# Where four weight blocks and the activations lie in SBUF, modulo 512 bytes

## The chip, the cores and the metric

The kernel runs on one core of a Trainium2 chip. The metric is the device time of one execution in microseconds. The kernel before took 2354.36 us, the median of three runs (2339.87 to 2354.72 us).

## What is computed

Two layers of an encoder over 512 positions of width 1024, all in float32. Each layer adds four sub-layers to x, each between an RMS norm ahead and one behind:

```python
x = x + 0.5 * rms_norm(swiglu(rms_norm(x, g[FFN1_PRE]), ffn_w_in[l, 0], ffn_w_out[l, 0]), g[FFN1_POST])
...
y = concat(rms_norm(ya), rms_norm(yb), rms_norm(yc))   # neighbourhood attention, Hyena, dilated attention
x = x + rms_norm(y @ w_out[l], g[MIX_POST])
xa = memory_cross_attn(rms_norm(x, g[XA_PRE]), rms_norm(mem, g[XA_MEM]), xa_wq[l], xa_wkv[l], xa_wo[l])
x = x + rms_norm(xa, g[XA_POST])
x = x + 0.5 * rms_norm(swiglu(rms_norm(x, g[FFN2_PRE]), ffn_w_in[l, 1], ffn_w_out[l, 1]), g[FFN2_POST])
```

The SwiGLU layers have 2816 hidden units; their weights and those of the projections are most of the work and all of the traffic that matters.

## The kernel before, in words

**Products in two parts.** The large products are made with float32r operands, each number split into a high part and the rest: high by high, low by high and high by low are summed in PSUM. ScalarE writes the high part of a weight block (`high`, line 306), VectorE subtracts it for the low part (`low`, line 311).

**The ring.** Weights arrive by DMA as blocks of 128 partitions by 1024 columns in `raw0` and `raw1`. They are split into `wh0` to `wh3` and `wl0` to `wl3`, a ring of four blocks: unit `u` uses block `u % 4`. A layer has 116 units. TensorE's `unit_done` frees a block for ScalarE, `split_ready` hands it to TensorE.

**Which operand is which.** In the first products of a stage (lines 453 to 455, and `products`, lines 397, 399 and 401, as `unit` calls it) 128 columns of a block are the stationary operand and 256 columns of `uH` or `uL` move. In the group loop of the two SwiGLU layers' first product (lines 501 to 503, `factor_product`) the hidden units are made in groups of two by seven quarter products: the groups' sums of weights are split into blocks 0, 1, 2 (two products each) and 3 (one product) counted from the stage's base, which is block 0 of the ring in the first FFN of a layer and block 2 in the second. The moving operand is `uH`, `uL` or one of `T1` to `T4`. In the output products (`out_tile`, which calls `products` twice with 512 columns, done as two halves of 256) it is the other way round: 128 columns of `hs` or `uH` are stationary and the block moves. `memory_values` has `memH` and `memL` stationary and a block moving. Each matmul instruction loads its stationary operand anew.

**Other matmuls.** The remaining ones, transposes against `eye` and the attention and Hyena products, are plain float32. Line 617 is apart: `KEEP_BUSY` matmuls whose result nobody reads multiply 128 columns of a block by 512 columns of the same block.

**Where things lie.** Tensors are allocated in order of the code, from low addresses to high, each start rounded up to 32 bytes where it is not there already. `xs`, `raw`, `wh`, `wl`, `tmp` (12,288 bytes of a partition), `side` (4096), then small ones: `stat`, two `yb` of 2048, `rsm`, `ones` (512), `eye` (512), `epsc`, `pr`, `negmax`, `den` and `rden` (256 each), `gss` (192). Then `gain_rows` (8192), `uH`, `uL` and a region of 90,112 bytes that the stages share and lay out anew: `hs`, `T1H` to `T4L`, `memH` and the attention's tensors all start a multiple of 512 bytes from `uH`. `pr` holds 106 columns of parameters and `ALIGN` columns that nobody uses; `ALIGN` is 106 before, so `pr` has 848 bytes.

The engines are synchronised by semaphores written out by hand; the order of the instructions of each engine is fixed in the code, and the two group loops run as hardware loops.

Of the kernel before, what the change touches and what calls it, by code (L numbers as in the profile page):

```python
# [10 lines left out]
F32R = mybir.dt.float32r  # L11
AX = mybir.AxisListType

P = 128
LAYERS = 2
D = 1024
# [41 lines left out]
RING, RAWS = 4, 2  # L58
# [4 lines left out]
IT_A, IT_C, IT_X, ITEMS = 0, 24, 48, 64  # L63
# [6 lines left out]

G0, CW0, CB0, SK0, NPAR = 0, 80, 98, 104, 106

ALIGN = 106
PRE = (0, 2, 5, 8)
POST = (1, 4, 7, 9)
G_GROUP, G_MEM = 3, 6
# [4 lines left out]
def build(nc, x, mem, par, grow, w_first, w_second, w_proj, rpb, t5, fw1, fw23, fw4, fvec, decay,  # L81
          k_emb, k_fwd, k_inv, k_time, k_namask, k_hot, k_lnn, k_eye, out):
    with ExitStack() as ctx:
        def sb(name, shape, dt=F32):
            return ctx.enter_context(nc.sbuf_tensor(name, shape, dt))
# [6 lines left out]

        xs = sb("xs", [P, NT, D])
        raw = [sb(f"raw{i}", [P, D]) for i in range(RAWS)]
        wh = [sb(f"wh{i}", [P, D], F32R) for i in range(RING)]
        wl = [sb(f"wl{i}", [P, D], F32R) for i in range(RING)]
        work = sb("tmp", [P, 6 * T])
        tmp = [work[:, i * T:i * T + T] for i in range(6)]
        yg = work[:, 0:D]
# [7 lines left out]
        eye = sb("eye", [P, P])  # L107
        epsc = sb("epsc", [P, 2])
        pr = sb("pr", [P, NPAR + ALIGN])
        negmax = sb("negmax", [P, ITEMS])  # L110
        den = sb("den", [P, ITEMS])
        rden = sb("rden", [P, ITEMS])
        gss = sb("gss", [P, 3, GROUPS])
# [1927 lines left out]
```

## Time and profile before

| | |
|---|---|
| median of 3 runs | 2354.36 us |
| lowest, highest | 2339.87, 2354.72 us |
| the profiled execution | 2339.08 us |
| its span, first to last instruction | 2337.3 us |
| granted TensorE clock, mean | 0.999 |
| matmuls | 19,236 |
| DMA, mean rate | 101 GB/s |

The span and what lies around it differ by 1.8 us. All terms are worked out against this one execution. TensorE's matmul durations in the profile overlap, since matmuls are pipelined and their ends are modelled: a stretch's length over the number of matmuls that start in it is the pace, and the recorded duration is that pace and a constant.

### The profile page before, as it was taken

How to read it: one execution, taken by the hardware profiler on the slowest of the kernel's cores; microseconds unless marked ns; L12 is line 12 of the kernel's file. 1: busy time of each engine (PE TensorE's matmuls, PEld its weight loads, DVE VectorE, ACT ScalarE, POOL GpSimd, SP SyncE). 2: the span in 40 equal slices, each digit the busy share in tenths (PEclk: the TensorE clock that was granted, in tenths of full speed). 3: DMA queues.
4: the chain of work that ended last, by engine and by line, in shares of the span. 5: the costliest groups of instructions: out<-in, count | busy, mean ns of one | idle time of the engine just before them, and what ended most of it. 6: DMA issues, size and time to landing. Idle time of an engine off the chain costs nothing.

```text
span 2337.3 us, 46573 instructions
## 1 busy us (share of the span) xinstructions
PE 2311.4 (99%) x19236; PEld 2251.4 (96%) x19236; DVE 1559.7 (67%) x2175; ACT 1051.6 (45%) x1733; POOL 114.6 (5%) x185
## 2 busy tenths in 40 slices
PE   7999999999999999999999999999999999999998
PEld 7999999998999999999999999989989989999998
DVE  7999437535365499993499983565364554999833
ACT  5445335227453464452454442442384444544422
POOL 0000000610000000000000000016000000000000
PEclk9999999999999999999999999999999999999999
DMA  4333323340234133333233332234202431322332
GB/s 140 109 114 122 116 82 135 82 138 19 73 118 136 55 109 110 120 110 94 71 128 113 119 109 91 93 121 124 90 1 85 146 114 46 125 102 100 113 98 75
DMA packets 66258, 236.54 MB, mean 101 GB/s; under 512 B 8882, under 2 KB 10632, under 8 KB 65600
## 3 DMA queue, kind: packets, MB, share of 16 engines
q1 hardware_dynamic: 57600, 209.74, 26.8%
q0 software_dynamic: 8224, 24.12, 3.2%
q8 instruction: 110, 1.80, 0.3%
q10 hardware_dynamic: 288, 0.59, 0.1%
q14 instruction: 36, 0.29, 0.0%
HBM read 232.29 MB, written 2.12 MB: 100 GB/s over the span
## 4 chain that ended last, share of the span: by engine, by line
PE 96%; ACT 1%; DVE 1%; issue 1%; DMA 0%; DVEq 0%; SPq 0%; ACTq 0%
PE bank L397 14%; PE bank L399 14%; PE bank L401 14%; PE bank L501 11%; PE bank L502 11%; PE bank L503 11%; PE bank L654 3%; PE bank L453 3%; PE bank L455 2%; PE bank L454 2%; PE bank L629 2%; PE bank L725 1%; PE bank L438 1%; PE bank L584 1%; PE bank L607 1%
## 5 line engine op out<-in xcount | busy, mean ns | idle before, releaser
L311 DVE TENSOR_TENSOR wl<-raw,wh 128x1024 fp32r<-128x1024 f32 x232 | 287.7, 1240 | 379.2 <-ACT wh L306 378.7
L306 ACT ACTIVATE wh<-raw 128x1024 fp32r<-128x1024 f32 x232 | 245.2, 1057 | 545.8 <-PE bank L401 474.4
L397 PE MATMUL bank<-wh,hs 128*128 128x256 f32 x1408 | 279.1, 279 | 0.1
L399 PE MATMUL bank<-wl,hs 128*128 128x256 f32 x1408 | 278.4, 279 | 0.0
L401 PE MATMUL bank<-wh,hs 128*128 128x256 f32 x1408 | 278.0, 278 | 0.0
L501 PE MATMUL bank<-uH,wh 128*128 128x256 f32 x960 | 266.5, 278 | 0.0
L503 PE MATMUL bank<-uH,wl 128*128 128x256 f32 x960 | 266.3, 277 | 0.0
L502 PE MATMUL bank<-uL,wh 128*128 128x256 f32 x960 | 266.3, 277 | 0.0
L397 PEld LDWEIGHTS bank<-wh,hs 128*128 128x128 f32 x1408 | 214.2, 188 | 0.6 <-issue 0.6
L401 PEld LDWEIGHTS bank<-wh,hs 128*128 128x128 f32 x1408 | 214.3, 188 | 0.0
L399 PEld LDWEIGHTS bank<-wl,hs 128*128 128x128 f32 x1408 | 214.1, 188 | 0.0
L1361 DVE TENSOR_TENSOR wl<-S,wh 128x1024 fp32r<-128x1024 f32 x160 | 194.5, 1216 | 0.0
L501 PEld LDWEIGHTS bank<-uH,wh 128*128 128x128 f32 x960 | 181.2, 189 | 0.9 <-issue 0.9
L503 PEld LDWEIGHTS bank<-uH,wl 128*128 128x128 f32 x960 | 180.3, 188 | 0.0
L502 PEld LDWEIGHTS bank<-uL,wh 128*128 128x128 f32 x960 | 180.2, 188 | 0.0
L952 ACT ACTIVATE wh<-S 128x1024 fp32r<-128x1024 f32 x80 | 85.2, 1065 | 157.7 <-DVE S L1349 136.4
L397 PE MATMUL bank<-uH,wh 128*128 128x256 f32 x768 | 154.5, 283 | 0.0
L399 PE MATMUL bank<-uL,wh 128*128 128x256 f32 x768 | 152.2, 280 | 0.0
L401 PE MATMUL bank<-uH,wl 128*128 128x256 f32 x768 | 152.1, 280 | 0.0
L453 PE MATMUL bank<-uH,wh 128*128 128x256 f32 x512 | 145.6, 284 | 3.3 <-DVE uL L1276 3.3
L454 PE MATMUL bank<-uL,wh 128*128 128x256 f32 x512 | 143.3, 280 | 0.0
L455 PE MATMUL bank<-uH,wl 128*128 128x256 f32 x512 | 143.3, 280 | 0.0
(268 smaller groups left out, 6068.8 us busy)
## 6 DMA issues: line engine op xcount, KB each, us to landing
raw<-in_w_proj SPq DMA_DIRECT2D x128, 512.0 KB, 3.5
raw<-in_w_first SPq DMA_DIRECT2D x96, 512.0 KB, 3.7
raw<-in_w_second SPq DMA_DIRECT2D x88, 512.0 KB, 3.5
side<-in_w_first SPq DMA_DIRECT2D x40, 512.0 KB, 3.6
raw_value<-in_w_first SPq DMA_DIRECT2D x40, 512.0 KB, 4.3
gain_rows<-in_grow POOLq DMA_DIRECT2D x15, 512.0 KB, 4.8
strip<-bias_of_distance POOLq DMA_DIRECT2D x2, 2688.0 KB, 11.0
strip<-in_rpb POOLq DMA_DIRECT2D x96, 24.0 KB, 2.2
```

Source lines behind the costliest of these rows:

```text
L306: e.activation(wh[u % RING][:], raw[u % RAWS][:], ACT.Copy).then_inc(high_ready, 1)
L311: e.tensor_tensor(wl[u % RING][:], raw[u % RAWS][:], wh[u % RING][:].bitcast(F32), ALU.subtract).then_inc(split_ready, 1)
L397: e.matmul(b[:, c], still_h, hi[:, c], start=first and c.start == 0, stop=False)
L399: e.matmul(b[:, c], still_h, lo[:, c], start=False, stop=False)
L401: mm = e.matmul(b[:, c], still_l, hi[:, c], start=False, stop=last and c.stop == n)
L453: e.matmul(bank[j][:, n], wh[u % RING][:, w], uH[:, k, n], start=half + k == 0, stop=False)
L454: e.matmul(bank[j][:, n], wh[u % RING][:, w], uL[:, k, n], start=False, stop=False)
L455: mm = e.matmul(bank[j][:, n], wl[u % RING][:, w], uH[:, k, n], start=False, stop=half == 1 and k == DT - 1)
L501: e.matmul(to, still_h, bH[:, k, :], start=k == 0, stop=False)
L502: e.matmul(to, still_h, bL[:, k, :], start=False, stop=False)
L503: mm = e.matmul(to, still_l, bH[:, k, :], start=False, stop=k == 3)
L1361: e.tensor_tensor(block_of(wl, base, n)[:, 0:cols], source, block_of(wh, base, n)[:, 0:cols].bitcast(F32), ALU.subtract).then_inc(low_done, 1)
```

## The change

Blocks 0 to 2 of `wh` and of `wl` get 16 columns (64 bytes) behind them that nobody uses, `negmax` moves from the small tensors to between `wh3` and `wl0` with 16 unused columns, and `ALIGN` goes from 106 to 10. No instruction, wait or transfer is added, removed or moved; only addresses change.

```diff
-ALIGN = 106
+
+PIECE = 16
+ALIGN = 10
...
-        wh = [sb(f"wh{i}", [P, D], F32R) for i in range(RING)]
-        wl = [sb(f"wl{i}", [P, D], F32R) for i in range(RING)]
+        wh = [sb(f"wh{i}", [P, D + (PIECE if i < RING - 1 else 0)], F32R)[:, 0:D] for i in range(RING)]
+        negmax = sb("negmax", [P, ITEMS + PIECE])[:, 0:ITEMS]
+        wl = [sb(f"wl{i}", [P, D + (PIECE if i < RING - 1 else 0)], F32R)[:, 0:D] for i in range(RING)]
...
-        negmax = sb("negmax", [P, ITEMS])
```

## Rows read from the trace of the kernel before

**Rows 1.** The page: busy time, share, instructions; the chain by engine.
```profile
PE 2311.4 (99%) x19236; PEld 2251.4 (96%) x19236; DVE 1559.7 (67%) x2175; ACT 1051.6 (45%) x1733; POOL 114.6 (5%) x185
PE 96%; ACT 1%; DVE 1%; issue 1%; DMA 0%; DVEq 0%; SPq 0%; ACTq 0%
```
**Rows 2.** Groups by line, operation, tiles (moving, then stationary) and shape; mean ns.
```profile
L397 PE MATMUL bank<-wh,hs 128*128 128x256 f32 x1408 | 279.1, 279 | 0.1
L501 PE MATMUL bank<-uH,wh 128*128 128x256 f32 x960 | 266.5, 278 | 0.0
L306 ACT ACTIVATE wh<-raw 128x1024 fp32r<-128x1024 f32 x232 | 245.2, 1057 | 545.8 <-PE bank L401 474.4 <-DMA raw<-in_w_proj 49.5 <-PE bank L503 11.3
...
L397 PE MATMUL bank<-uH,wh 128*128 128x256 f32 x768 | 154.5, 283 | 0.0
...
L453 PE MATMUL bank<-uH,wh 128*128 128x256 f32 x512 | 145.6, 284 | 3.3 <-DVE uL L1276 3.3
...
L397 PE MATMUL bank<-wh,uH 128*128 128x256 f32 x512 | 102.8, 281 | 0.0
...
L501 PE MATMUL bank<-T2H,wh 128*128 128x256 f32 x320 | 88.8, 277 | 0.0
...
L397 PE MATMUL bank<-memH,wh 128*128 128x256 f32 x128 | 36.0, 281 | 0.0
```
**Rows 3.** Windows: stretch, length, PE busy (matmuls), granted clock, DMA share, GB/s.
```profile
66.00:235.00 169.00, 169.00 (x1494) 1.00 0.33 115
240.00:347.00 107.00, 107.00 (x947) 1.00 0.31 98
853.00:1042.00 189.00, 189.00 (x1670) 1.00 0.31 108
1175.00:1383.00 208.00, 208.00 (x1837) 1.00 0.33 114
468.00:523.00 55.00, 55.00 (x469) 1.00 0.41 139
1047.00:1160.00 113.00, 113.00 (x962) 1.00 0.29 93
1388.00:1509.00 121.00, 121.00 (x1031) 1.00 0.27 87
1621.00:1676.00 55.00, 55.00 (x469) 1.00 0.41 141
2008.00:2204.00 196.00, 196.00 (x1666) 1.00 0.30 104
2210.00:2328.00 118.00, 118.00 (x1005) 1.00 0.27 88
```
**Rows 4.** Timeline of TensorE from 1046.2 us: start, us, merged instructions.
```profile
1046.22 0.48 PE L397 MATMUL bank<-wh,hs 128*128 128x256 f32 x2
1046.54 0.39 PE L399 MATMUL bank<-wl,hs 128*128 128x256 f32 x2
```
**Rows 5.** Lines 617, 779, 629, 501, 397: duration ns min/median/max.
```profile
L617 PE MATMUL bank<-wh x30: 393/397/504, 531.3 to 1691.1; 128*128 128x512 f32 x30
...
L779 PE MATMUL bank<-inv,taps x64: 377/379/379, 446.7 to 1605.9; 128*128 128x256 f32 x64
...
L629 PE MATMUL bank<-eye,tmp x352: 270/273/331, 532.1 to 1933.2; 128*128 128x128 f32 x176
...
L501 PE MATMUL bank<-T1H,wh x320: 276/276/281, 46.9 to 2201.2; 128*128 128x256 f32 x160
...
L397 PE MATMUL bank<-wh,hs x1408: 276/279/365, 235.9 to 2329.6; 128*128 128x256 f32 x176
```
**Rows 6.** Waits: who waited for whom, us in total, times, longest.
```profile
ACT wh L306 <- PE bank L401: 474.4, 120, 6.5
```

## The prediction

> **What bounds the kernel now.** I read the head of the page first: TensorE is busy for 99% of the span, VectorE for 67%, ScalarE for 45%, and the chain of work that ended last lies on TensorE for 96% of the span [rows 1]. So what the change is worth is read from TensorE's rhythm alone.
>
> The listing of groups by line and shape shows what fills it [rows 2]: matmuls of 128x128 weights against 256 moving columns, all on operands split into a high and a low part. With the sibling rows of each (three per line family, twelve of x320, six of x128) they are 3 x 1408 + 3 x 960 + 12 x 320 + 3 x 768 + 3 x 512 + 3 x 512 + 6 x 128 = 17,088 of the 19,236 matmuls. In every one of them one operand is a weight block of the ring, the other an activation (uH, uL, T1 to T4, hs, memH, memL). These are the pairs whose distance the change sets.
>
> A recorded matmul duration is no rhythm, since matmuls overlap; so I took windows with nothing else in them and divided length by count [rows 3]. About two of each count are matmuls cut by the edges. 853 to 1042 us: 189 us / 1668 = 113.3 ns. 2008 to 2204 us: 196 us / 1664 = 117.8 ns. Those two windows run the same code, the same products of the group loop. The ten windows fall on these two paces and none between: four **fast** (5948 matmuls, 113.3 ns), six **slow** (5602, 117.8 ns). Granted clock is 1.00 in all, the DMA share much the same (0.27 to 0.41, with a fast and a slow window both at 0.30).
>
> How a pace begins can be seen at 1046 us [rows 4]: after a wait the first pair of a line starts 0.32 us before the pair of the next line, and from then to 1160 us all is slow, where 853 to 1042 us was fast [rows 3]. So the pace is a lock between the weight loads and the moving stream that a restart sets and that then holds for a whole stage. Every matmul has a weight load of its own.
>
> What would no lock cost? Durations help, because the tail in them is constant. A 128-column float32 transpose, two passes, is 273 ns; fast matmuls are 276, slow ones 279 to 281 [rows 5]. The pace of the transposes is 109.2 ns by the same offset (276 stands for 113.3, 281 for 117.8; so 273 for about 109 to 110). Hence 17,088 matmuls carry about 4 ns each at the fast and 8.6 ns at the slow pace that is not columns: about 110 us in all. This is the sum the change can touch.
>
> The Trainium skill, TensorE: Matmul & The Clock Gate, section Back-to-back issue gap, gives N/2.4 + 2.5 ns, that is 109.2 ns for 256 columns. The trace's windows lie above it at both paces. The same skill in SBUF — State Buffer, section SBUF: two separate sides, says that contention is structural and that TensorE's ports wait for nobody. By that, addresses are worth nothing; it is the ground of a rival below.
>
> **The change part by part.**
> Addresses, counted from the shapes in the code with starts rounded up to 32 bytes. Before, from the first high block to uH: 8 x 4096 (blocks) + 12288 + 4096 (tmp, side) + 96 + 2 x 2048 + 32 + 512 + 512 + 32 (stat to epsc) + 864 (pr) + 3 x 256 + 192 + 8192 bytes = 64,448 = 126 x 512 - 64. So all eight blocks lie 64 bytes behind a multiple of 512 from uH: one piece, for all. After: 192 + 192 bytes behind the blocks and 256 + 64 for negmax between them come in, 256 of negmax and 384 of pr go out: net + 64. The blocks lie 0, 1, 2 and 3 pieces behind. So the change does what it says; block 1 alone keeps its distance. Where a block is the moving operand and hs, uH or memH the stationary one, the distance has the other sign. Before, both signs show both paces (240 to 347 and 1047 to 1160 us are one line with hs stationary [rows 3]), so the sign costs nothing that shows.
>
> Who uses which block: the group loop's seven products use its blocks 2, 2, 2 and 1 times, starting at block 0 in two of the four FFNs and at block 2 in the others; of its 6720 matmuls blocks 0 and 2 get 1920 each, 1 and 3 get 1440 each. The other 10,368 are shared evenly, 2592 each. Block 0: 4512, block 1: 4032, block 2: 4512, block 3: 4032.
>
> *Distance 0.* The trace has one row at it: line 617 multiplies a block by itself, 512 columns in one instruction. Its durations are 393 at least and 397 in the median, against 377 to 379 for a float32 matmul with the same 512 column passes, line 779 [rows 5]. That is 16 to 18 ns for one weight load, where distance 1 shows 3 to 8. Upper end: a 256-column matmul pays all of it, 10 to 12 ns above today's mean, x 4512 = +45 to +54 us. Lower end: half of it belongs to the second 256 columns, 8 to 9 ns, which is the slow pace; then only those that are fast today lose, half of 4512 x 4.5 ns = +10 us. I take the lower end: a stream of 256 columns under one load each is nearest to the rows of distance 1, and the 30 matmuls of line 617 stand in threes, each run just after a restart.
>
> *Distances 2 and 3.* No row has them. Bounds: no extra at all, 115.6 - 109.2 = 6.4 ns x 8544 = -55 us; or the price of distance 0 in full, 11 x 8544 = +94 us. Nearest is distance 1, whose two signs pay the same; I take the same two paces in equal shares: 0.
>
> *The locks.* Within a stage the block changes every 12, 24 or 48 matmuls, and with it the distance. A lock could no longer hold over 1666 matmuls. Taken one by one that redraws the pace often; with a fast and a slow share of half each today it moves the sum little. Bounds: all slow gone, (5602 + half of the 5538 outside the windows) x 4.5 = -38 us; all fast gone, (5948 + 2769) x 4.5 = +39 us.
>
> *The rest, together.* tmp, eye, side and the small tensors move by the same 192 bytes against a multiple of 512, so transposes keep their distances. Line 654 (values in the region, tmp moving) changes by 128 bytes: 704 matmuls, a few ns at most, within 3 us either way. No instruction, wait, DMA or semaphore is added. Writes into the blocks could change length (1057 ns on ScalarE); ScalarE waits 474 us in all for the matmuls to free the blocks [rows 2, 6], so this is covered; uncovered, 5% of one write would be 50 ns at 232 places, 12 us.
>
> **Sum.** 2339.1 us of the profiled execution + 10 + 0 + 0 = 2349 us. The profile is at the low end of the runs shown (2339.9 to 2354.7, median 2354.4). Their distance, 14.8 us, is 3300 matmuls x 4.5 ns: two FFN loops that fall into the other lock. So 2349 is no change from the median.
>
> **The rivals.**
> *Nothing depends on the address.* The lock is one of time alone, and padding only moves bytes. For it: the two paces come up at one and the same distance. Against it: line 617, at another distance, has a third price [rows 5]. It gives what the runs of before give, 2339 to 2355 us, within 1% too. Chance 0.06. The rule of the Trainium skill's SBUF — State Buffer named above would have it so; the two paces at one clock show that something does hold TensorE up, though not that it is the address.
> *Slower: block 0 meets its activations.* In place: every product of ring block 0. Price 10 to 12 ns x 4512: 2339 + 50 = 2389 us. For it: line 617, 30 of 30 matmuls above the free pass. It decides from +31 us over the low end, that is from 7 ns more per matmul of block 0, if 2 and 3 stay as distance 1. Were 2 worse too, 2400 and over. Chance 0.32.
> *Faster: larger distances keep the streams apart.* Blocks 2 and 3 at 109.2 ns, 0 at the lower end: 2339 - 55 + 10 = 2294 us; or only the slow lock breaks at each change of block and the fast one holds: 2339 - 38 = 2301 us. For it: 110 us of extra exist, and the same code runs 1837 matmuls at the fast pace. Against it: the slow lock is as durable, 1666 in one loop [rows 3]. Chance 0.32.
>
> **How the numbers follow.** A measurement of this kernel tells about 1% from no change. Forecast, paces as today and block 0 slow: 0.30; with the first rival 0.36 within 1%, where the forecast's own range is 2331 to 2378. Slower rival 0.32, faster rival 0.32. Both signs hold most of the chance, so the range takes in most of both: 2295 to 2395, leaving out a clean win of 60 us and a price of distance 0 that spreads to block 2.
>
> **What the profile after would show.** The same windows divided by count: stretches of 24 matmuls of one block each with its own pace. Right: 113.3 and 117.8 in all four blocks. Slower rival: block 0 alone at 122 or more, durations of 285 and up. Faster rival: durations of 273 in blocks 2 and 3, or no long stretch at 117.8. Line 617 must stay at 393 to 397, since both its operands move together. I am wrong if block 1, whose distance stays, changes its pace by more than a redraw, or if TensorE's share falls below 98% of the span.

## The result, and the profile after

The changed kernel took 2376.16 us in the median (2375.67 to 2378.83, 4 runs), the kernel before 2354.54 us (2339.87 to 2356.65, 4 runs): ratio 1.0117, 95% interval 1.0087 to 1.0146. It is slower by 1.2%. The forecast was no change, 2349 us; the time lies in the range, on the side of the slower rival (2389 us), whose chance was 0.32. The profiled execution has a span of 2373.9 us against 2337.3, 36.6 us more. Its runs also differ by 3 us only, where those of before differ by 17. In the experiments below one execution of u2 (4482 us at a granted clock of 0.91) and one of u3 (2749 us at 0.78) count in the medians, which they move by 0.5 us at most, and not in the ratios.

The head of the page after: busy time of each engine, then the chain by engine.

```profile
PE 2348.3 (99%) x19236; PEld 2289.0 (96%) x19236; DVE 1561.8 (66%) x2175; ACT 1052.8 (44%) x1733; POOL 114.7 (5%) x185
PE 96%; ACT 1%; DVE 1%; issue 1%; DMA 0%; DVEq 0%; SPq 0%; ACTq 0%
```

Beside [rows 1]: the same instructions, shares within a point, and 36.9 us more on TensorE. TensorE's idle time has not changed: 25.9 us before, 25.6 after. Line numbers are two higher after. As before, "fast" is the pace of 113.3 ns a matmul and "slow" that of 117.8; a piece is 64 bytes. The windows (stretch, length, TensorE busy and matmuls, granted clock, DMA share, GB/s) answer to [rows 3]:

```profile
100.00:200.00 100.00, 100.00 (x846) 1.00 0.30 106
250.00:340.00 90.00, 90.00 (x768) 1.00 0.32 100
870.00:1060.00 190.00, 190.00 (x1611) 1.00 0.29 105
2050.00:2240.00 190.00, 190.00 (x1611) 1.00 0.31 106
2250.00:2360.00 110.00, 110.00 (x939) 1.00 0.27 86
```

Less the two matmuls at the edges: 118.5, 117.5, 118.1, 118.1 and 117.4 ns. Before, three of the four group loops ran at 113.3. Now all four run above 118. From the first to the last matmul of line 501 to 503, the four loops took 771.5 us before and 796.7 after: +25.2 of the 36.6 us. The four output stages took 498.5 and 501.5: +2.9. The other 8.5 us are left, by subtraction, for the remaining products.

A mean hides the blocks, so I read one turn of the group loop. These timeline rows (start, length of one, instruction) are the first matmul of each block: the ring's block 2, then 3, 0 and 1 in the second FFN of a layer; 24, 24, 24 and 12 matmuls lie between them. First before, where the distances are all one piece:

```profile
948.12 0.28 PE L501 MATMUL bank<-uH,wh 128*128 128x256 f32 x1
...
950.84 0.28 PE L501 MATMUL bank<-T2H,wh 128*128 128x256 f32 x1
...
953.56 0.28 PE L501 MATMUL bank<-T3H,wh 128*128 128x256 f32 x1
...
956.28 0.28 PE L501 MATMUL bank<-T4H,wh 128*128 128x256 f32 x1
...
957.64 0.28 PE L501 MATMUL bank<-uH,wh 128*128 128x256 f32 x1
```

2.72, 2.72, 2.72 and 1.36 us: 113.3 ns in every block. The same turn after:

```profile
968.83 0.28 PE L503 MATMUL bank<-uH,wh 128*128 128x256 f32 x1
...
971.67 0.28 PE L503 MATMUL bank<-T2H,wh 128*128 128x256 f32 x1
...
974.50 0.28 PE L503 MATMUL bank<-T3H,wh 128*128 128x256 f32 x1
...
977.38 0.28 PE L503 MATMUL bank<-T4H,wh 128*128 128x256 f32 x1
...
978.75 0.28 PE L503 MATMUL bank<-uH,wh 128*128 128x256 f32 x1
```

2.84 us for block 2 (118.3 ns), 2.83 for block 3 (117.9), 2.88 for block 0 (**120.0**) and 1.37 for block 1 (114.2). In the two FFNs whose base is block 0 the order is 0, 1, 2, 3, and there block 1 is slow too (117.9). Over all four loops the means of the blocks 0 to 3 are 119.9, 116.6, 118.4 and 117.8 ns, against 114.6, 114.2, 114.6 and 114.9 before.

The same can be done for the whole kernel: the order of the program says which block each of the 17,088 products uses, and the time from its start to that of the next one is its pace.

| block | distance after, pieces | ns before | ns after | x matmuls, us |
|---|---|---|---|---|
| 0 | 0 | 115.9 | 119.7 | +17 |
| 1 | 1, as before | 115.7 | 117.0 | +5 |
| 2 | 2 | 115.7 | 118.6 | +13 |
| 3 | 3 | 116.0 | 116.7 | +3 |

These are 38 us, against the 36.6 of the span. Blocks 0 and 2 have 30 of them. Block 3 is slow where it is stationary (117.8 ns), and faster than before where it moves: 114.3 ns in the output stages of the FFNs, 116.8 before.

Line 617 (619 after) was to stay at 393 to 397 ns, and within 3 ns it did; the wait of ScalarE that covers the writes is there as in [rows 6]:

```profile
L619 PE MATMUL bank<-wh x30: 390/398/500, 544.1 to 1725.8; 128*128 128x512 f32 x30
```
```profile
ACT wh L308 <- PE bank L403: 482.1, 121, 6.5
```

### The profile page after: what moved, and what is told of

It is laid out like the page before. It is cut to its first block, busy times and chain, and to the rows that moved or that the text cites. A ratio compares the mean times of both kernels' runs of the same rounds, so it can differ in the third digit from the quotient of the medians.

```text
span 2373.9 us, 46573 instructions
## 1 busy us (share of the span) xinstructions
PE 2348.3 (99%) x19236; PEld 2289.0 (96%) x19236; DVE 1561.8 (66%) x2175; ACT 1052.8 (44%) x1733; POOL 114.7 (5%) x185
## 4 chain that ended last, share of the span: by engine, by line
PE 96%; ACT 1%; DVE 1%; issue 1%; DMA 0%; DVEq 0%; SPq 0%; ACTq 0%
PE bank L399 14%; PE bank L401 14%; PE bank L403 14%; PE bank L503 11%; PE bank L504 11%; PE bank L505 11%; PE bank L656 3%; PE bank L455 3%; PE bank L457 2%; PE bank L456 2%; PE bank L631 2%; PE bank L727 1%; PE bank L440 1%; PE bank L586 1%; PE bank L609 1%
## 5 line engine op out<-in xcount | busy, mean ns | idle before, releaser
L504 PE MATMUL bank<-uL,wh 128*128 128x256 f32 x960 | 270.9, 282 | 0.0
L503 PE MATMUL bank<-uH,wh 128*128 128x256 f32 x960 | 270.8, 282 | 0.0
L505 PE MATMUL bank<-uH,wl 128*128 128x256 f32 x960 | 270.6, 282 | 0.0
L399 PE MATMUL bank<-uH,wh 128*128 128x256 f32 x768 | 155.5, 284 | 0.0
L401 PE MATMUL bank<-uL,wh 128*128 128x256 f32 x768 | 153.1, 281 | 0.0
L403 PE MATMUL bank<-uH,wl 128*128 128x256 f32 x768 | 153.0, 281 | 0.0
L455 PE MATMUL bank<-uH,wh 128*128 128x256 f32 x512 | 146.6, 286 | 3.3 <-DVE uL L1278 3.3
L457 PE MATMUL bank<-uH,wl 128*128 128x256 f32 x512 | 144.3, 282 | 0.0
L456 PE MATMUL bank<-uL,wh 128*128 128x256 f32 x512 | 144.3, 282 | 0.0
```

The source lines that it names most:

```text
L399: e.matmul(b[:, c], still_h, hi[:, c], start=first and c.start == 0, stop=False)
L401: e.matmul(b[:, c], still_h, lo[:, c], start=False, stop=False)
L403: mm = e.matmul(b[:, c], still_l, hi[:, c], start=False, stop=last and c.stop == n)
L455: e.matmul(bank[j][:, n], wh[u % RING][:, w], uH[:, k, n], start=half + k == 0, stop=False)
L456: e.matmul(bank[j][:, n], wh[u % RING][:, w], uL[:, k, n], start=False, stop=False)
L457: mm = e.matmul(bank[j][:, n], wl[u % RING][:, w], uH[:, k, n], start=False, stop=half == 1 and k == DT - 1)
```

## The experiments

Two theories at the start. **A, each block pays for its own distance.** **B, a ring with one distance holds either pace whatever the distance is, and changing from block to block costs.** All times below are medians of 4 to 12 executions; each ratio is to the kernel before on the same chip, whose own median lay between 2340 and 2350 us, differently on each chip.

### One distance for all blocks: 0, 2, 3, 4

```diff
-ALIGN = 106
+ALIGN = 122   # u0; u2: 90, u3: 74, u4: 58
```

> All eight blocks at distance 0 (ALIGN 122). Theory A, the price lies in the distance of each block: all 17,088 float32r matmuls run as those of block 0 after, 119 to 120 ns, so 15,000 to 17,000 x 4 ns over the mean of before: 2405 to 2425 us. Theory B, the price lies in changing the distance from block to block, any single distance holds either lock: 2339 to 2356 us, windows at 113.3 or 117.8 ns. Theory C, only the columns of one 256-column half count as at line 617: 124 ns and more, 2470 us and over.

> All blocks at distance 2 (ALIGN 90). Theory A: as block 2 after, 118.4 ns in the group loop, 2375 to 2390 us. Theory B: 2339 to 2356 us, two paces.

> All blocks at distance 3 (ALIGN 74). Theory A: as block 3 after, 117.8 ns as the stationary and 114.3 ns as the moving operand, 2355 to 2375 us. Theory B: 2339 to 2356 us, two paces.

> All blocks at distance 4 (ALIGN 58), half of 512 bytes, which the change does not use. Theory A: a pace of its own, somewhere from 109 to 120 ns, the same with either operand stationary since 4 and -4 are one distance: 2230 to 2425 us. Theory B: 2339 to 2356 us, two paces.

| distance, pieces | time, us | ratio (95%) |
|---|---|---|
| 0 | 2408.39 | 1.0259 (1.0219 to 1.0298) |
| 2 | 2388.28 | 1.0174 (1.0123 to 1.0224) |
| 3 | 2359.67 | 1.0043 (1.0020 to 1.0066) |
| 4 | 2408.48 | 1.0259 (1.0220 to 1.0299) |

Windows of a group loop and of the last output stage, at distance 0:

```profile
66.00:235.00 169.00, 169.00 (x1407) 1.00 0.30 105
2240.00:2330.00 90.00, 90.00 (x753) 1.00 0.31 100
```

at distance 2:

```profile
66.00:235.00 169.00, 169.00 (x1426) 1.00 0.31 106
2240.00:2330.00 90.00, 90.00 (x761) 1.00 0.31 100
```

at distance 3:

```profile
66.00:235.00 169.00, 169.00 (x1437) 1.00 0.31 107
1080.00:1160.00 80.00, 80.00 (x681) 1.00 0.29 93
2240.00:2330.00 90.00, 90.00 (x797) 1.00 0.31 96
```

and at distance 4:

```profile
66.00:235.00 169.00, 169.00 (x1411) 1.00 0.31 106
2240.00:2330.00 90.00, 90.00 (x752) 1.00 0.32 100
```

Counted start to start over the whole stage, all four group loops are at 120.0 ns at distances 0 and 4, at 118.7 at distance 2 and at 117.8 at distance 3. None of the four has a fast loop. At distance 3 two of the four output stages are fast, the first and the last (797 in 90 us, 113.3 ns); the two between are slow (681 in 80 us, 117.8). There the block moves, so that the stationary operand begins three pieces ahead of it, which is one behind modulo four. Theory A holds for one distance at a time, and B falls as it was put: one distance for all does not give either pace. The forecast of u0 was 2405 to 2425 us, and its theory C (124 ns and more) falls too. That u4 equals u0 to 0.1 us was not forecast by anything.

### The control, the period, and half pieces

c1 keeps the order of tensors of after without its distances; u5 is ALIGN = 42, x05 ALIGN = 114, x15 ALIGN = 98 in the kernel before.

Parts of c1's edit:

```diff
# c1, against after
...
-D + (PIECE if i < RING - 1 else 0)
+D
-negmax = sb("negmax", [P, ITEMS + PIECE])[:, 0:ITEMS]
+negmax = sb("negmax", [P, ITEMS + 64])[:, 0:ITEMS]
...
-ALIGN = 10
+ALIGN = 42
```

> Control: negmax stands between the high and the low blocks as after (with 64 unused columns), no padding between blocks, ALIGN 42: all blocks at distance 1. Distance theory: the places of negmax, tmp and side are worth nothing, 2337 to 2358 us, windows at 113.3 or 117.8 ns. Rival, the moved small tensors cost: 2370 us and over.

> All blocks at distance 5 (ALIGN 42 in the kernel before). Theory of a period of 256 bytes, since distances 0 and 4 gave the same: as distance 1, 2337 to 2358 us with the two paces. Theory of a period of 512 bytes with a mirror (0 and 4 alike by chance): as distance 3, 2350 to 2362 us, or a pace not seen yet.

> All blocks 32 bytes behind (ALIGN 114), half a piece. If whole pieces of 64 bytes decide (uH begins within the piece ahead): the paces of distance 1 or of 0, 2337 to 2358 or 2408 us. If the cost goes on smoothly: 117 ns and some 2375 us.

> All blocks 96 bytes behind (ALIGN 98), one piece and a half. Whole pieces: the paces of distance 1 or of 2, 2337 to 2358 or 2388 us. Smooth: between them, some 2370 us.

c1: 2337.40 us, ratio 0.9994 (0.9967 to 1.0020): the moved negmax, tmp and side cost nothing that shows in an interval of 0.3% either way. u5: 2339.42 us, 1.0005 (0.9974 to 1.0036), with both paces:

```profile
66.00:235.00 169.00, 169.00 (x1493) 1.00 0.33 115
870.00:1050.00 180.00, 180.00 (x1591) 1.00 0.31 111
2050.00:2190.00 140.00, 140.00 (x1191) 1.00 0.29 105
```

So 5 is 1 as 4 is 0: what counts is the distance modulo **256** bytes. x05: 2371.44 us, 1.0128 (1.0088 to 1.0169); x15: 2385.31 us, 1.0190 (1.0149 to 1.0231). Their paces are 118.3 ns (group loops) and 116.7 (output stages) at half a piece, 117.3 to 118.7 and 120.0 at one and a half. They are paces of their own and not those of a whole piece, so the cost goes by less than 64 bytes. Half a piece comes out at the time expected of a smooth course (some 2375 us). One and a half does not: some 2370 us were expected, between distances 1 and 2, and its ratio is not below that of distance 2 (1.0174).

### Block 0 alone, at distance 0 and at distance 2

Parts of b0's edit (that of `wl` is the same as that of `wh`):

```diff
# b0, against after: block 0 at distance 0, blocks 1 to 3 at 1
...
-D + (PIECE if i < RING - 1 else 0)
+D + (PIECE if i == 0 else 0)
...
-ITEMS + PIECE
+ITEMS + 3 * PIECE
...
-ALIGN = 10
+ALIGN = 42
```

b2 has `3 * PIECE if i == 0 else 0`, `ITEMS + PIECE` and ALIGN = 106: block 0 at distance 2, the others at 5. p5 has `4 * PIECE if i == 1 else 0`, `ITEMS` and ALIGN = 106: distances 1, 1, 5, 5.

> Block 0 alone at distance 0, blocks 1 to 3 at 1, which is the case in which the sum of the prediction took +10 us. If each block pays for its own distance: 4512 matmuls at 120.0 instead of 115.8 ns, +19 us over the kernel before of the same chip, blocks 1 to 3 at 113.3 or 117.8. If a change of distance breaks the fast pace in the other blocks too: theirs near 117.8 as well, +19 + 6300 x 4.45 ns = +47 us at most.

> Block 0 alone at distance 2, blocks 1 to 3 at distance 5, which ran as distance 1. If it is distance 0 that breaks the fast pace in the blocks after it: blocks 1 to 3 of the group loop at 113.3 in three loops of four, and 4512 x 2.9 ns = +13 us. If any block with another distance breaks it: blocks 1 to 3 at 117.8, +13 and some +20 us.

> Blocks 0 and 1 at distance 1, blocks 2 and 3 at distance 5: the distance changes modulo 512 and not modulo 256. Period of 256 bytes and nothing for the change: the fast pace holds across the blocks, within 8 us of before. If a change modulo 512 breaks the fast pace: 117.8 throughout, +30 us.

b0: 2378.21 us, 1.0174 (1.0141 to 1.0207), 36 us over the kernel before of its chip, about as slow as the change itself, with one block at distance 0 and nothing at 2 or 3. Its turn of the group loop, blocks 2, 3, 0, 1:

```profile
969.89 0.28 PE L503 MATMUL bank<-uH,wh 128*128 128x256 f32 x1
...
972.71 0.28 PE L503 MATMUL bank<-T2H,wh 128*128 128x256 f32 x1
...
975.54 0.28 PE L503 MATMUL bank<-T3H,wh 128*128 128x256 f32 x1
...
978.42 0.28 PE L503 MATMUL bank<-T4H,wh 128*128 128x256 f32 x1
...
979.83 0.28 PE L503 MATMUL bank<-uH,wh 128*128 128x256 f32 x1
```

2.82, 2.83, 2.88 and 1.41 us: block 0 at 120.0 ns, and the three blocks at distance 1 all at 117.5 to 117.9. In all four loops they are slow. Over the whole kernel, counted as in the table above, block 0 costs 18 us more than in the kernel before and the three others 21 together. b2 tells whether any change of distance does that. It took 2346.34 us, 1.0017 (0.9991 to 1.0042):

```profile
956.20 0.28 PE L503 MATMUL bank<-uH,wh 128*128 128x256 f32 x1
...
958.92 0.28 PE L503 MATMUL bank<-T2H,wh 128*128 128x256 f32 x1
...
961.64 0.28 PE L503 MATMUL bank<-T3H,wh 128*128 128x256 f32 x1
...
964.48 0.28 PE L503 MATMUL bank<-T4H,wh 128*128 128x256 f32 x1
...
965.86 0.28 PE L503 MATMUL bank<-uH,wh 128*128 128x256 f32 x1
```

2.72, 2.72, 2.84 and 1.38 us: block 0 pays 118.3 ns, and blocks 2 and 3 behind it are **fast**, block 1 nearly (115). This is so in all four loops, and its ten runs lie within 1.1 us where those of before spread over 28. So a block at another distance does not just break the pace: in the group loops of these two kernels it settles that of the three others, slow with distance 0, fast with distance 2. (In the plain products, lines 397 to 401 with a block stationary, b0's three others run at 116.1 to 117.2 ns in the mean, both paces.) That the block just ahead decides is not shown, and the change speaks against it: in its second FFNs block 1 comes right behind block 0 and runs at 114.0 ns, in the same place of b0 at 117.8, and the two kernels differ in blocks 2 and 3 alone. The output stages of b2, where the block moves, are at 118.0 to 118.3. p5: 2345.32 us, 0.9999 (0.9964 to 1.0034); its group loops are at 113.6, 117.8, 117.6 and 113.4 ns: a step of 256 bytes between blocks leaves a fast loop fast.

### hs two pieces further

Part of one line:

```diff
-("below_hs", [P, FT * T], F32)
+("below_hs", [P, FT * T + 32], F32)
```

> hs 128 bytes (two pieces) further on: in the output products of the four FFNs the stationary hs now lies one piece behind the moving block, as a stationary block lies behind uH, instead of one ahead. If the sign counts (stationary behind the moving operand: both paces; ahead: slow as a rule): up to 3 of the 4 stages go from 117.7 to 113.3 ns, 3 x 1056 x 4.45 = -14 us. If it does not: as before, within 3 us.

2325.28 us, 0.9939 (0.9911 to 0.9966), which is 14 us and the size expected. The profile does not carry the reason:

```profile
66.00:230.00 164.00, 164.00 (x1450) 1.00 0.32 114
250.00:340.00 90.00, 90.00 (x797) 1.00 0.32 101
1070.00:1150.00 80.00, 80.00 (x681) 1.00 0.30 94
2230.00:2320.00 90.00, 90.00 (x767) 1.00 0.24 79
```

The first output stage is fast and the three later ones are slow (117.8), as in [rows 3]. That execution took 2335.6 us, 10 over the median. The gain is measured; that it comes from the output stages is not shown.

### One matmul of 512 columns for two of 256

```diff
-halves = [slice(c, c + HALF) for c in range(0, n, HALF)]
+halves = [slice(0, n)]
```

w0 has ALIGN = 122 besides; wb has w1's edit and `FT * T + 16` ahead of hs.

> Distance 1, and the products of lines 397 to 401 as one matmul of 512 columns instead of two of 256: half as many weight loads there (4416 fewer). If the price is one of the load: 215.8 + 4 to 9 ns for 512 columns instead of 226.7 or 235.6, some -40 us. If it is one of the columns: 226 to 236 ns, within 10 us of before.

> As w1, but all blocks at distance 0. Price of the load: 215.8 + 10.8 = 227 ns for 512 columns, 2375 us or less. Price of the columns: 240 ns as twice 120, some 2408 us. Line 617 showed 231 to 240 ns.

> w1 with hs 64 bytes further on, so that in the output products the stationary hs lies at distance 0 from the moving block, which for 512 columns in one matmul gave 226.7 ns where w1 gave 227.3 to 229.7 ns: 2112 matmuls x 1 to 2 ns, 2 to 5 us below w1, 2313 to 2316 us. Rival, distance 0 costs as with 256 columns: no gain or a loss against 2318 us.

w1: 2317.76 us, 0.9911 (0.9885 to 0.9938). w0: 2356.09 us, 1.0076 (1.0049 to 1.0103). wb: 2328.97 us, 0.9916 (0.9886 to 0.9946). A window of w0's output stage, whose matmuls have 512 columns:

```profile
250.00:340.00 90.00, 90.00 (x399) 1.00 0.32 105
```

and of w1's:

```profile
250.00:340.00 90.00, 90.00 (x395) 1.00 0.30 96
```

Start to start, w0 takes 226.7 to 227.5 ns, where two matmuls of 256 at distance 0 take 240.0: 11 ns over 215.8, the pace of line 779 in the same trace (float32, 512 column passes), as 10.8 over 109.2 for 256 (line 629, 256 column passes). At distance 0 the price is one **of the weight load**, not of the columns. At distance 1 it is less clean: 226 to 232 ns with hs or uH stationary, 233 with a block stationary, so 11 to 18 ns a load where 256 columns paid 4 or 8.6, and -21 us by the ratio came out instead of -40. wb got the 226.6 to 227.0 ns it was made for, but its group loops, with 256 columns as ever, run at 115.6 ns in the mean against 113.5 in w1, both paces against one. Its runs go from 2313 to 2337 us, w1's from 2317 to 2319. It misses its 2313 to 2316 us; within the intervals the two are the same, and both beat the kernel before.

## Why the prediction was wrong

**What bounds the kernel: right.** TensorE's rhythm alone; the same instructions and clock, the same idle time of TensorE, and all of the 36.6 us in its busy time.

**Two paces set by a restart and held: right, and too small a picture.** They are the two paces of one distance. The runs of before took 2322 to 2358 us over the chips used, a spread that stretches of 4.5 ns a matmul allow. That the pace is a lock between weight loads and moving stream was argued; no run shows it.

**Addresses: right.** The change does what it says, and c1 shows no cost of the rest of it within 0.3%.

**Distance 0: mis-sized, the lower end a little too low.** The step took 8 to 9 ns over the free pass, half of line 617's 16 to 18, and +10 us. It is 10.8 ns, a pace of 120.0: 4512 x (120.0 - 115.8) = +19 us, where 115.8 is the mean pace of all 17,088 products before, and +17 in the change itself. The reason given, that part of line 617's price belongs to its second half, is wrong as well: w0 pays the same 11 ns with 512 columns. Why line 617 pays more, 16 to 18 ns in [rows 5], stays open; its matmuls come in threes behind a restart.

**Distances 2 and 3 put at distance 1's paces, 0 us: the step that failed.** No row had them. Distance 2 has a pace of 118.7 ns: 4512 x 2.9 = +13 us, and +13 in the change. Distance 3 has 117.8 as the stationary operand and both paces as the moving one, +3 us in the change. The ground was that the two signs of distance 1 pay the same, read out of one fast output stage in [rows 3]; in u3 no group loop is fast at three pieces, where three of four are at one. That is one profile.

**The locks: wrong in kind, and the smaller part here.** The step said that frequent changes redraw the pace evenly, 0 us. In b0 and b2 they settle it: the blocks at distance 1 (or 5, which is the same) were slow in every loop of b0 and fast or nearly so in every loop of b2. In the change only block 1 can show this, since its distance stays: +5 us. So b0's like total is no proof of the change's cause: of b0's loss 21 us lie on three blocks still at distance 1, of the change's 13 on block 2 at distance 2 and 5 on block 1. The sign of being wrong that was named, block 1 changing by more than a redraw, can't be read: it went to 117.9 ns in the loops of the first FFNs, where it had run at 113.3 and 113.8, and a redraw could give that too.

**The sum** began at the profiled 2339.1 us, 15 under the median, so that its +10 read as no change. With the terms as measured it is 2339 + 17 + 16 + 5 = 2377 us, against 2376.

**The slower rival** had the place right and the price too high: 10 to 12 ns a matmul of block 0 where it was 4.2. It counted nothing for the other blocks, and the two errors nearly cancel, 2389 against 2376 us. The faster rival fell: no window of any run is below 113.3 ns. The 109.2 ns that the Trainium skill's formula for an isolated matmul gives for 256 columns (TensorE: Matmul & The Clock Gate, section Back-to-back issue gap) is not reached by these products at any distance tried.

**The rival that nothing depends on the address** fell with u0 and u4, 58 us slower by 16 columns of padding more or 48 fewer alone. The Trainium skill, SBUF — State Buffer, section SBUF: two separate sides, has TensorE's ports wait for nobody. These runs show TensorE's pace hang on where its own two operands lie, 113.3 to 120.0 ns; they don't bear on waits for other engines.

What stays open is the mechanism itself: why 256 bytes are the period, why distance 1 has two paces, and which mix and order of distances makes the fast one last.

## What to carry to other kernels

Where every float32r matmul loads its own weights and TensorE is the bound, as here, the start of the stationary against the moving operand modulo 256 bytes is worth a try: from 113.3 to 120.0 ns a matmul hung on padding alone. Judge it on windows divided by counts and block by block, not on one run's time, since one distance can have two paces. A setting that no row shows should not be put at the price of its neighbour: one run with all blocks at distance 2 would have given 118.7 ns. And blocks can't always be summed one by one. Their own distances give 19 + 13 us and up to 8 for block 3 in the change, near the 37 measured, but 19 in b0, where the medians differ by 36, and 13 in b2, where 4 came out (-2 to +10).

## What the runs showed of the hardware

Pace of a float32r matmul, 128x128 weights, 256 columns, each with its load, by how far the stationary operand begins behind the moving one, modulo 256 bytes:

| bytes behind | ns a matmul | where |
|---|---|---|
| 0 | 120.0 | u0, u4 |
| 32 | 118.3 | x05, group loops |
| 64 | 113.3 or 117.8 | before, u5; u3, output stages |
| 96 | 117.3 or 118.7 | x15, group loops |
| 128 | 118.7 | u2 |
| 160 | 120.0 | x15, output stages |
| 192 | 117.8, seldom 113.3 | u3, group loops; before, output stages |
| 224 | 116.7 | x05, output stages |

Float32 matmuls show no such price where the padding moved one operand against the other: line 654 keeps 111.7 to 112.1 ns for 128 columns in the kernels before, after, u0, u2 to u5, x05 and x15. Line 629, whose operands kept their distance, is at 109.2 ns. And ten runs of b2 lie within 1.1 us, where the kernel before spreads over 21 to 28 us on one chip.
